# The block inverse of a chunked linear recurrence: odd heads change the partition half with every level, and TensorE adds the old inverse

## The reference, cut to what matters

```python
def rwkv7_recurrence(r, decay, k, v, a_vec, b_vec):
    """All (B, S, H, N). State S_t (B,H,N_v,N_k):
    S_t = S_{t-1} diag(w_t) + (S_{t-1} a_t) b_t^T + v_t k_t^T ;  y_t = S_t r_t."""
    def step(state, inp):
        r_t, w_t, k_t, v_t, a_t, b_t = inp
        sa = jnp.einsum('bhvk,bhk->bhv', state, a_t)
        state = (state * w_t[:, :, None, :] + sa[..., None] * b_t[:, :, None, :]
                 + v_t[..., None] * k_t[:, :, None, :])
        return state, jnp.einsum('bhvk,bhk->bhv', state, r_t)
```

## Time and profile before

| | |
|---|---|
| median of 3 runs | 2029.79 us |
| the profiled execution | 2032.83 us, its span 2030.7 us |
| mean granted TensorE clock | 0.97 |
| TensorE busy | 1876.2 us (92%), 11708 matmuls and 11708 weight loads |
| VectorE, ScalarE, GpSimd busy | 891.1, 692.4, 203.0 us |
| first chain (windows 0 and 1) | 1489.27 to 1516.13 us of the span |
| second chain (windows 2 and 3) | 1547.09 to 1573.43 us |

### The profile page before, as it was taken

One profiled execution on the slowest core, in us unless ns is written; L12 is line 12 of the kernel. 1 busy time (PEld: TensorE's weight loads), 2 busy tenths in 40 slices (PEclk: granted clock), 3 DMA queues, 4 the chain that ended last, 5 costly groups with the idle time before them and its releaser, 6 DMA issues. The chain is left out here.

```text
span 2030.7 us, 27890 instructions
## 1 busy us (share of the span) xinstructions
PE 1876.2 (92%) x11708; PEld 1445.0 (71%) x11708; DVE 891.1 (44%) x1446; ACT 692.4 (34%) x1127; POOL 203.0 (10%) x165
## 2 busy tenths in 40 slices
PE   5999988989999998999999988999498899999999
PEld 2666655758888885888888866666288578888887
DVE  5266866364434345333333342333755543332332
ACT  3215546242323233332223243545522333222321
POOL 0023434200000001000000200333100020000000
PEclk9999989989999998999999998999799999999999
DMA  9672100212222321233223212111000123322231
GB/s 370 217 256 80 39 20 32 73 52 94 94 93 97 98 97 52 94 105 102 75 103 120 69 64 78 44 42 32 0 4 4 33 83 104 109 90 92 94 123 43
DMA packets 44477, 176.17 MB, mean 87 GB/s; under 512 B 5568, under 2 KB 5824, under 8 KB 41024
## 3 DMA queue, kind: packets, MB, share of 16 engines
q1 hardware_dynamic: 44352, 174.38, 25.2%
HBM read 168.33 MB, written 2.10 MB: 84 GB/s over the span
## 5 line engine op out<-in xcount | busy, mean ns | idle before, releaser
L342 PE MATMUL bank<-hs,wsp 128*128 128x512 f32 x1368 | 549.7, 402 | 21.2 <-DVE hs L1458 11.5
L1009 ACT ACTIVATE wsp<-ring 128x1024 fp32r<-128x1024 f32 (+2 forms) x244 | 268.7, 1104 | 853.2 <-PE bank L344 851.5
L343 PE MATMUL bank<-hs,wsp 128*128 128x512 f32 x1368 | 538.8, 394 | 0.0
L344 PE MATMUL bank<-hs,wsp 128*128 128x512 f32 x1368 | 538.3, 393 | 0.0
L1419 DVE TENSOR_TENSOR wsp<-ring,wsp 128x1024 fp32r<-128x1024 f32 (+2 forms) x244 | 312.1, 1281 | 406.4 <-ACT wsp L1009 406.3
L342 PEld LDWEIGHTS bank<-hs,wsp 128*128 128x128 f32 x1368 | 260.7, 191 | 103.9 <-issue 42.1
L344 PEld LDWEIGHTS bank<-hs,wsp 128*128 128x128 f32 x1368 | 260.5, 190 | 55.8
L343 PEld LDWEIGHTS bank<-hs,wsp 128*128 128x128 f32 x1368 | 260.7, 191 | 54.3 <-issue 1.9
L344 PE MATMUL bank<-hids,wsp 128*128 128x512 f32 x608 | 241.0, 396 | 0.0
L343 PE MATMUL bank<-hids,wsp 128*128 128x512 f32 x608 | 241.0, 396 | 0.0
L342 PE MATMUL bank<-hids,wsp 128*128 128x512 f32 x608 | 241.0, 396 | 0.0
(11 more groups left out here) (305 smaller groups left out, 1934.3 us busy)
## 6 DMA issues: line engine op xcount, KB each, us to landing
ring<-m_gate SPq DMA_DIRECT2D x44, 512.0 KB, 3.4
ring<-m_up SPq DMA_DIRECT2D x44, 512.0 KB, 3.4
ring<-m_down SPq DMA_DIRECT2D x32, 704.0 KB, 4.1
ring<-m_w_in SPq DMA_DIRECT2D x38, 512.0 KB, 3.5
arena<-ada_late SPq DMA_DIRECT2D x16, 1024.0 KB, 6.5
ring<-m_w_up SPq DMA_DIRECT2D x32, 512.0 KB, 3.4
ring<-m_w_down SPq DMA_DIRECT2D x32, 512.0 KB, 3.4
ring<-m_w_out SPq DMA_DIRECT2D x16, 512.0 KB, 3.6
```

What stands on the lines that cost most here:

```text
L342: pe.matmul(out, lhs[0], rhs[0], start=start, stop=False)
L343: pe.matmul(out, lhs[0], rhs[1], start=False, stop=False)
L344: return pe.matmul(out, lhs[1], rhs[0], start=False, stop=stop)
L1009: act.activation(wsp[:, s % SPLIT, 0, 0:size], ring[:, i % RING, 0:size], ACT.Copy)\
```

## The change

Each odd head now changes its half of the partitions with every level: what is read on rows r is written to the other half. Even heads stay. So one step uses all four quarters: (0,0) and (1,1) for the even heads, (0,1) and (1,0) for the odd ones. VectorE cannot add an old inverse on one half to a new one on the other, so for odd heads TensorE does it: a product with a 64x64 identity carries the old inverse over, and the product with the power is accumulated onto it in PSUM. Even heads still go through VectorE's addition. The odd heads' first inverse (identity + A) is now made by TensorE too, as a step `inverse(w, 0)`. It counts six inverse steps of a window where there were five.

PSUM tiles are cut by even and odd: ScalarE copies the even heads' powers and transposed powers (one instruction of 2 x 256 columns) and the odd heads' inverse (256 columns). VectorE copies the odd heads' powers and adds the even heads' inverse (256 columns). Powers and transposed powers of one window are now one step on TensorE, and `chains` interleaves them with the inverse steps, one level behind. Two semaphores, `tanh` and `sig_g`, become one, `squashed`.

```diff
-            def chain(w, lv):
+            def powers(w, lv):
 
                 q, d = w % 2, 12 * (w // 2) + w % 2 + 1
                 now = PP[q][:, lv % 2, :, :]
...
+                def powT(r, e, c):
+                    return AT[q][half(r), e, c * P:c * P + CHUNK] if lv == 0 else now[half(r), 1, cols(4 * e + c)]
+
+                pe.wait_ge(S("power_odd"), d + 2 * lv)
                 if lv == 0:
                     pe.wait_ge(S("pairs"), 8 * (w // 2) + 2 * q + 2)
...
-                                mm = pe.matmul(bank[half(j), 3 * q, cols(4 * e + c)], powT(j, e, c),
-                                               now[half(j), 0, cols(4 * e + c)], start=True, stop=True)
-                    mm.then_inc(S("power_full"), 1)
+                else:
+                    pe.wait_ge(S("power_even"), 10 * (w // 2) + 2 * (lv - 1) + q + 1)
+                claim(4 * q, "power_even", 10 * (w // 2) + 2 * lv + q + 1)
+                claim(4 * q + 1, "power_odd", d + 2 * (lv + 1))
+                for c in range(4):
+                    for r, to in HALVES:
+                        e = int(r != to)
+                        mm = pe.matmul(bank[half(to), 4 * q + e, cols(c)], powT(r, e, c), now[half(r), 0, cols(4 * e + c)],
+                                       start=True, stop=True)
                 if lv < 4:
...
-                if lv >= 1:
-                    pe.wait_ge(S("inverse"), d + 2 * (lv - 1))
-                    claim(3 * q + 2, "inverse", d + 2 * lv)
-                    for e in range(2):
-                        for c in range(4):
-                            for j in range(2):
-                                mm = pe.matmul(bank[half(j), 3 * q + 2, cols(4 * e + c)], now[half(j), 0, cols(4 * e + c)],
-                                               TT[q][half(j), cols(4 * e + c)], start=True, stop=True)
-                    mm.then_inc(S("inverse_full"), 1)
+                    for c in range(4):
+                        for r, to in HALVES:
+                            e = int(r != to)
+                            mm = pe.matmul(bank[half(to), 4 * q + e, cols(4 + c)], now[half(r), 0, cols(4 * e + c)],
+                                           powT(r, e, c), start=True, stop=True)
+                mm.then_inc(S("power_full"), 1)
+
+            def inverse(w, lv):
+
+                q, d = w % 2, 12 * (w // 2) + w % 2 + 1
+                pe.wait_ge(S("power_odd"), d + 2 * lv)
+                if lv:
+                    pe.wait_ge(S("power_even"), 10 * (w // 2) + 2 * (lv - 1) + q + 1)
+                    pe.wait_ge(S("inverse_even"), d + 2 * (lv - 1))
+                    pe.wait_ge(S("inverse_odd"), d + 2 * (lv - 1))
+                    claim(4 * q + 2, "inverse_even", d + 2 * lv)
+                claim(4 * q + 3, "inverse_odd", d + 2 * lv)
+                for c in range(4):
+                    for r, to in HALVES:
+                        if r != to:
+                            old = TT[q][half(r), cols(4 + c)] if lv else const("ident64")[half(r), :]
+                            pe.matmul(bank[half(to), 4 * q + 3, cols(c)], const("ident64")[half(r), :], old,
+                                      start=True, stop=False)
+                            mm = pe.matmul(bank[half(to), 4 * q + 3, cols(c)], PP[q][half(r), lv % 2, 0, cols(4 + c)], old,
+                                           start=False, stop=True)
+                        elif lv:
+                            mm = pe.matmul(bank[half(to), 4 * q + 2, cols(c)], PP[q][half(r), lv % 2, 0, cols(c)],
+                                           TT[q][half(r), cols(c)], start=True, stop=True)
+                mm.then_inc(S("inverse_full"), 1)
+
+            def chains(w):
+                for lv in range(6):
+                    if lv < 5:
+                        powers(w, lv)
+                    if lv:
+                        inverse(w + 1, lv - 1)
+                    if lv < 5:
+                        powers(w + 1, lv)
+                    inverse(w, lv)
+                inverse(w + 1, 5)
```

On VectorE the first inverse loses its odd half:

```diff
-                for e in range(2):
-                    ins = dve.tensor_tensor(heads4(TT[q][:, 256 * e:256 * e + 256]), heads4(AT[q][:, e, :])[:, :, 0:CHUNK],
-                                            const("ident64")[:, None, :].to_broadcast([P, 4, CHUNK]), ALU.add)
+                dve.tensor_tensor(heads4(TT[q][:, 0:256]), heads4(AT[q][:, 0, :])[:, :, 0:CHUNK],
+                                  const("ident64")[:, None, :].to_broadcast([P, 4, CHUNK]), ALU.add)\
```

More of the change, by code:

```diff
@@ L763, in first_power @@
                 for e in range(2):
-                    claim(banks[e], "power", v)
+                    claim(banks[e], "power_odd", v)
                 for c in range(4):
@@ L811, in chain @@
-                if lv < 4:
-                    claim(3 * q + 1, "powerT", 8 * (w // 2) + 2 * lv + q + 1)
-                    for e in range(2):
[L814 to L818, removed]
@@ L918, in _ @@
             key_values(1, 5)
-            for lv in range(6):
-                chain(0, lv)
-                chain(1, lv)
+            chains(0)
             solve(0, (0, 1))
@@ L943, in _ @@
             key_values(3, 4)
-            for lv in range(6):
-                chain(2, lv)
-                chain(3, lv)
+            chains(2)
             solve(2, (0, 1))
@@ L958, in _ @@
             pe.wait_ge(S("wkv"), 8)
-            pe.wait_ge(S("sig_g"), 1)
+            pe.wait_ge(S("squashed"), 2)
             for c in range(4):
@@ L1855, in chain @@
[L1855 to L1864, removed]
+                ins.then_inc(S("power_odd"), 1)
@@ new lines, in first_power, with chains @@
+                own("power_odd")
+                dve.tensor_tensor(heads4(TT[q][:, 0:256]), heads4(AT[q][:, 0, :])[:, :, 0:CHUNK],
+                                  const("ident64")[:, None, :].to_broadcast([P, 4, CHUNK]), ALU.add)\
+                   .then_inc(S("inverse_even"), 1)
+                own("inverse_even")
+            def chains(w):
+                for lv in range(6):
+                    for x in (w, w + 1):
+                        q = x % 2
+                        if lv < 5:
+                            n = 2 if lv < 4 else 1
+                            dve.wait_ge(S("power_full"), 12 * (w // 2) + 2 * (lv + 1) + q + 1)
+                            dve.tensor_copy(PP[q][:, (lv + 1) % 2, 0:n, 256:512],
+                                            bank[:, 4 * q + 1, 0:256 * n].rearrange("p (a n) -> p a n", a=n))\
+                               .then_inc(S("power_odd"), 1)
+                            own("power_odd")
+                        if lv - 1 + q >= 1:
+                            inverse_even(w + 1 - q, lv - 1 + q)
+                inverse_even(w + 1, 5)
```

54 lines of the change are left out of this document (28 added, 26 removed).

## The result

The changed kernel takes 2042.5 us (median of 6 runs, 2039.08 to 2045.63). The kernel before takes 2032.72 us in the six runs that now stand for it. The ratio is 1.0053, with a 95% interval of 1.0036 to 1.0070: slower, by about 10.8 us by the ratio and 9.8 by the medians. The forecast was 2041.4 us, +11.6.

A forecast was written before the change was run, and what follows sets the result against it. TensorE's instruction blocks, about 3.8 us each, were taken to bound the changed chains: +11.9 us for the chains, -0.7 for the first inverse, +0.4 behind the chains, +11.6 on 2029.8, so 2041.4 us, range 2035 to 2047.

The forecast's parts named there:

- What bounds the kernel: In the two chains, array pace and instruction blocks (about 128 loads per 3.8 us) lie side by side; the changed chain is instruction-bound.
- The chains: The two recurrence chains: 8.9 blocks each for 7.1, taking 32.5 and 32.6 us for 26.86 and 26.34, together +11.9 us.
- Array: TensorE's array time in a chain: 19.6 us for 26.2, with power steps and inverse steps at 0.935 us each.
- Copies and waits at no cost: VectorE's and ScalarE's copies and TensorE's new waits in the chains stay hidden; window 1's first powers cost under 0.1 us.
- The first inverse: Ahead of both chains VectorE loses one of two 0.44 us additions in four places: -0.7 us, bounds -0.4 and -1.0.
- What follows the chains: Behind each chain, `solve` uses up the open block and TensorE stops 0.7 (0.9) us: +0.4 us, bounds 0 and +1.6.
- The array decides: Rival: blocks come ahead in time, chains take 19.6 us each, kernel 2015 us; chance 0.08.
- Blocks come faster: Rival: a block takes 3.2 us in a steady run, chains 27.7 and 27.8 us, kernel 2032 us; chance 0.05.
- the third rival: Granted clock falls in the stops to 1.2 GHz, chains 39.2 us each, +26 us, kernel 2055 us; chance 0.02.

## Why the prediction was right

**What bounds the kernel.** That the array and the instruction blocks lay side by side in the chain was the step on which all rested. The run without identity products shows it: TensorE's busy time fell by more than a third, and the chain's length stayed as before. The times of the packets show why: each block has a delay of its own of about 3.7 us. The forecast had the size of that limit and its unit right, and took it for a steady supply.

**The number.** The median came out 1.1 us above the forecast 2041.4, and that is in part luck: the forecast stood on a base of 2029.8 us, the median of the three runs at hand, and with six runs the base is 2.9 us higher, while the change is 9.8 to 10.8 us and not 11.6.

**The chains.** Forecast +11.9 us (32.5 and 32.6); measured +10.6 (31.25 and 32.54) in the profile. The first was 1.3 us over. The 8.9 blocks are right (2286 and 2283 records against an estimate of 1141 loads, 2282), and so are eight blocks inside each chain; the block was priced at 3.8 us and took 3.72 between the stops of the first chain and 3.79 in the second. The eight blocks from the first edge on took 29.2 us in the first chain and 29.7 in the second, for the forecast 30.4: the first of them, behind an edge without a stop, took only 3.1 and 3.2. That the second chain hit its 32.6 all the same is luck: what follows its last edge took 2.48 us (1582.23 to 1584.71) for 1.8, with the granted clock at 0.83 there.

**Array.** 16 products in 0.467 us, as taken from the kernel before. The inverse step can be read where no stop falls into it: one starts at 1502.05 and the next, with a power step of 32 products between, at 1504.02. That is 1.97 us, and less 0.935 for the powers an inverse step took 1.0 us, for the forecast 0.935. Under the stops this cost nothing. That the array needs the same time for 16 columns as for 64, in both runs with fewer columns, stood in no expectation.

**Copies and waits at no cost.** No stop of TensorE in a chain was ended by VectorE or ScalarE. ScalarE's work rose from 5.4 to 10.4 us a chain and stayed beside it.

**The first inverse.** Forecast -0.7 us. The stretch ahead of the first chain is 12.49 us before and 11.9 after. The shifted run, which adds 32 products there, has 11.6. In the three other profiles with the change's version of VectorE's list it is 11.9 as well, and 12.4 to 12.5 in all five with VectorE's full first inverse. Together with the stretch between (-0.6) this term was nearer -1.2, though that stretch holds moved edges too.

**What follows the chains.** Forecast +0.4; the stretch after the second chain was 0.2 us shorter.

**The rivals.** "The array decides" is out. "Blocks come faster" is out for the changed kernel, where they came 3.72 and 3.79 us apart on the mean, though single ones came in 3.1 to 3.4. The granted clock did what the third rival said, but for a moment only. Around the end of the second chain of the changed kernel (1584.71) there is this stretch:

```profile
1583.00:1587.00 4.00, 4.00 (x122) 3.92 (x120) 0.88 (x3) 0.80 (x3) 0.00 (x0) 0.61 0.02 4
```

It cost at most 2 us, part of it in the place of a stop. In the run with one identity product and in the one without, the granted clock was below 1 in the stretch between the chains, and these are runs whose kernels gained less than their chains. What makes the clock fall for so short a time in one run and not in another stays open.

The Trainium skill ("Runtime: NRT & Kernel Launch", "Instruction fetch mechanics") says of a block's edge that its cost is mostly hidden. In the changed kernel the trace agrees at the first of the nine edges of the first chain and not at the other eight, where TensorE stands still for up to 1.6 us.

## What to carry to other kernels

Before packing small products onto more of the array, count the instructions: in this kernel TensorE got 256 of them in about 3.8 us, 15 ns each, and a float32 product on a quarter needs four. A chain that is busy all the time can still be at that limit, and then less time on the array gives nothing while every added instruction costs 15 ns. Nor does a pause before it help for long: behind a slower stretch the first edge was free and the second already had a stop. Look for "issue" stops at equal counts anywhere in the trace, each a little over a microsecond behind an instruction packet, and first merge products that share their weights; the extra quarters pay after that.

## What the runs showed of the hardware that was not expected

- In both runs with 16 instead of 64 columns the granted clock fell to the half level 11 and 14 us into the chain, though TensorE issued as many instructions as with 64, and the chains got longer by it (34.1 for 31.25 us, 35.95 for 26.86). TensorE had been busy for the whole 14 us in the one, and for 8.2 of 11.3 us in the other. Why it fell stays open.
- At full clock a 64x64 product with 16 columns took as long as one with 64: 0.93 us for 16 of them on two quarters, 0.48 us on four. With 128 columns 16 of them took 1.69 us on two quarters.
- An instruction packet starts only after TensorE has passed the edge before, and TensorE goes on 1.2 to 1.6 us after its end.
- A block took 3.7 us on the mean in one run and 3.9 in another of nearly the same list, and 4.0 with one identity product for four. Single ones took 3.0 to 4.8.
